# Channel projections placed between the attention steps of a hybrid layer, on one PSUM bank

## What is computed

```python
h = rms_norm(x, norm_w)
proj = jnp.einsum('bsd,de->bse', h, w_in)
q, kv_all, gate_logits, nsa_z, cv_h, cv_b, cv_c, cv_z = jnp.split(proj, SPLIT_POINTS, axis=-1)
...
o_nsa = (gates[..., 0:1] * unblock(o_cmp) + gates[..., 1:2] * unblock(o_slc)
         + gates[..., 2:3] * unblock(o_win))
o_nsa = o_nsa.reshape(B_, S_, D_NSA) * jax.nn.silu(nsa_z)
u = cv_c * cv_h
conv = lax.conv_general_dilated(u, conv_w[:, None, :], ...) + conv_b     # width 3, causal
o_conv = cv_b * conv * jax.nn.silu(cv_z)
mix = jnp.concatenate([o_nsa, o_conv], axis=-1)
return x + jnp.einsum('bse,ed->bsd', mix, w_out)
```

## Time and profile before

| | |
|---|---|
| time, median of 3 runs | 781.68 us (779.86 to 785.8) |
| the profiled execution | 780.35 us, its span 778.4 us |
| PE busy | 705.4 us, 91% of the span |
| DVE, ACT, POOL busy | 460.3, 370.0, 195.9 us |
| mean granted clock of PE | 0.989 |

### The profile page before, as it was taken

How to read it: one execution, slowest core, us unless ns; L and a number is a source line. 1 busy time by engine, 2 the same in 40 slices (tenths; PEclk the granted TensorE clock), 3 DMA queues, 4 the chain that set the end, 5 groups by cost and what they waited for, 6 DMA issues and landing times.

```text
span 778.4 us, 11020 instructions
## 1 busy us (share of the span) xinstructions
PE 705.4 (91%) x3951; PEld 587.8 (76%) x3951; DVE 460.3 (59%) x958; ACT 370.0 (48%) x891; POOL 195.9 (25%) x212
## 2 busy tenths in 40 slices
PE   2899999799999999999967778999999999999877
PEld 2888899698788888888856566777778777777755
DVE  4776462724200514033167888888898888888751
ACT  5643536432221111201046876767676766766640
POOL 2112635421122212222133532012111122222310
PEclk9999999999999999999987999999999999999999
DMA  6421122211111121120021200000000000000101
GB/s 204 163 82 41 48 75 60 55 55 41 41 41 55 43 53 43 52 55 13 1 81 61 103 1 0 24 5 28 28 19 10 29 28 28 28 28 29 55 28 54
DMA packets 17909, 36.75 MB, mean 47 GB/s; under 512 B 2496, under 2 KB 2752, under 8 KB 17856
## 3 DMA queue, kind: packets, MB, share of 16 engines
q1 hardware_dynamic: 17856, 36.05, 15.0%
HBM read 31.85 MB, written 4.19 MB: 46 GB/s over the span
## 4 chain that ended last, share of the span: by engine, by line
PE 64%; DVE 21%; ACT 7%; issue 4%; DMA 2%; POOL 1%; SPq 0%; ACTq 0%; DVEq 0%
PE pj L975 13%; PE pj L976 13%; PE pj L977 13%; DVE ptl L934 4%; PE po L1141 4%; PE tp L1161 4%; PE po L1142 3%; PE sc L1065 3%; PE sc L1064 2%; PE pout L975 2%; DVE nmax L927 2%; ACT pth L637 2%; DVE p_sel L915 2%; PE pout L976 2%; PE pout L977 2%
## 5 line engine op out<-in xcount | busy, mean ns | idle before, releaser
L368 POOL TENSOR_TENSOR wl<-raw,wh 128x512 fp32r<-128x512 f32 (+1 forms) x68 | 92.2, 1368 | 255.7 <-ACT wh L454 255.7
L975 PE MATMUL pj<-hh,wh 128*128 128x512 f32 x352 | 137.2, 390 | 0.0
L977 PE MATMUL pj<-hh,wl 128*128 128x512 f32 x352 | 137.0, 389 | 0.0
L976 PE MATMUL pj<-hl,wh 128*128 128x512 f32 x352 | 136.9, 389 | 0.0
L637 ACT CAST pth<-tp 128x512 fp32r<-128x512 f32 (+1 forms) x148 | 86.4, 587 | 78.1 <-PE tp L1161 77.0
L934 DVE TENSOR_TENSOR ptl<-tp,pth 128x512 fp32r<-128x512 f32 (+1 forms) x148 | 101.6, 687 | 30.3 <-ACT pth L637 28.5
L426 POOL TENSOR_SCALAR p_win<-p_win,precip,gate 128x64 f32<-128x64 f32 x64 | 36.6, 572 | 195.3 <-DVE precip L909 195.1
L1141 PE MATMUL po<-pth,val 128*128 128x512 f32 x132 | 64.7, 490 | 19.8 <-DVE ptl L934 17.7
L975 PE MATMUL pj<-wh,hh 128*128 128x256 f32 (+1 forms) x256 | 75.7, 296 | 7.0 <-POOL wl L368 5.8
L454 ACT CAST wh<-raw 128x512 fp32r<-128x512 f32 (+1 forms) x68 | 41.9, 626 | 80.2 <-PE pj L977 76.1
L977 PEld LDWEIGHTS pj<-hh,wl 128*128 128x128 f32 x352 | 66.1, 188 | 13.9
(11 more groups left out here) (173 smaller groups left out, 1434.1 us busy)
## 6 DMA issues: line engine op xcount, KB each, us to landing
raw<-in_wpack SPq DMA_DIRECT2D x64, 256.0 KB, 2.7
ub<-in_x SPq DMA_DIRECT2D x8, 512.0 KB, 3.4
wor<-in_wout SPq DMA_DIRECT2D x8, 512.0 KB, 3.3
xo<-in_x SPq DMA_DIRECT2D x16, 256.0 KB, 2.6
out<-xo SPq DMA_DIRECT2D x16, 256.0 KB, 2.0
raw<-in_wpack SPq DMA_DIRECT2D x4, 280.0 KB, 3.1
mixc<-in_normw SPq DMA_DIRECT2D x1, 512.0 KB, 6.3
maskb<-in_maskc SPq DMA_DIRECT2D x1, 448.0 KB, 5.6
```

Of the source, the lines that this page charges most:

```text
L368: nc.gpsimd.tensor_tensor(wl[e % 2][:, j * w:(j + 1) * w], raw[p % 4][:, 0:w], wh[e % 2][:, j * w:(j + 1) * w].bitcast(F32), ALU.subtract)\
L975: MM(dst, lh, rh, start=start, stop=False)
L976: MM(dst, lh, rl, start=False, stop=False)
L977: return MM(dst, ll, rh, start=False, stop=stop)
```

## The change

ENTRIES ends with the first z. The second z and the channel entries become 18 side tiles of 128 columns (TILES), each two groups of eight products, one for each half of the tokens. They are done in the attention steps, on the one bank `pf`, which the output projection uses after them. SIDE says how many products stand in each step, before and after the turned tiles; the loop behind it then puts together whole groups in the first 88 steps: one group of eight before the first scores, then one in every second step up to 33, and one in every third from 36 to 87. The output projection's 128 products follow from step 89, mostly 3, 3 and 2 in a step. There are 136 steps in place of 151.

UNITS now runs from the first query tile to the last. The weights of the side tiles come in halves of 512 columns (`fraw`, two buffers; `fh` and `fl`, three). ACT rounds one half in each step with a group, POOL subtracts. The first tap of the convolution is ACT's now, two remain with DVE. The output weights are loaded and split in steps 88 to 91, two in each, the second of each two by DVE. The last output tile takes its channel half first for both column halves. The key transposes of the window stand between the items of the first z. Memory is laid out anew, and the 280-column entry comes in five pieces.

```diff
-UNITS = [(i, g) for i in reversed(range(NT)) for g in range(GROUPS)]
+UNITS = [(i, g) for i in range(NT) for g in range(GROUPS)]
...
+SIDE = [(2, 2)] * 34 + [(2, 1), (2, 1), (2, 0)] * 18 + [(0, 0)] + [(1, 1)] * 4
+SIDE += [(2, 1), (2, 1), (2, 0)] * ((NS - len(SIDE)) // 3 + 2)
+SIDE = SIDE[:NS + 6] + [(4, 0)] * 4
+
+behind = 0
+for step in range(88):
+    behind += sum(SIDE[step])
+    SIDE[step] = (behind // 8 * 8, 0)
+    behind %= 8
...
+            def side(f):
+
+                kind, t, _ = TILES[f // 2]
+                cols = slice(f % 2 * 512, (f % 2 + 1) * 512)
+                if kind in ("z", "cz"):
+                    act.wait_ge(f_done, f + 1)
...
+                    A(th[:, :], pf[:, :], ACT.Tanh, scale=0.5).then_inc(f_tanh, 1)
+                elif kind == "ch":
+                    act.wait_ge(f_done, f + 1)
+                    nc.scalar.copy(mixc[:, t, cols], pf[:, :]).then_inc(f_free, 1)
+                elif kind == "cc" and f % 2 == 1:
+                    act.wait_ge(f_free, f + 1)
+                    A(mixc[:, t, :], ub[:, 2:2 + SEQ], ACT.Identity, scale=prm[:, P_CW + 3 * t + 2:P_CW + 3 * t + 3],
+                      bias=prm[:, P_CB + t:P_CB + t + 1]).then_inc(conv_first, 1)
...
                 for kind, _ in turned[:1]:
                     prob_hi(kind)
+                for f in side_ends(k, 0):
+                    if f < NF:
+                        side(f)
                 u = output_at(k)
...
+                for h in halves_at(k):
+                    half_hi(h)
+                for j in wout_at(k):
+                    act.wait_ge(wor_in[j % 2], 16 * (j // 2 + 1))
+                    act.wait_ge(f_done, NF)
+                    nc.scalar.copy(woh[:, KT_ORDER[j], :], wor[j % 2][:, :]).then_inc(woh_ready, 1)
...
+            def channels(p):
+
+                f, k = divmod(p, 8)
+                n, hf = divmod(f, 2)
+                if k == 0 and f >= 1:
+                    pe.wait_ge(f_free, f)
...
+                ins = three(pf[:, :], fh[h % 3][:, c], fl[h % 3][:, c], hh[:, k, s], hl[:, k, s], k == 0, k == NK - 1)
...
-                m, part = part_at(k)
-                if m is not None:
-                    output(m, part)
+                for p in side_parts(k, 0):
+                    channels(p) if p < OUT_0 else output(p)
                 for t in turned[1:]:
                     turn(n, *t)
+                for p in side_parts(k, 1):
+                    channels(p) if p < OUT_0 else output(p)
                 if k + 1 < NS:
                     scores(k + 1)
```

More of the change, by code:

```diff
@@ L47 @@
 ENTRIES = [("q", 0, 256, 0), ("kc", 512, 256, 0), ("q", 256, 256, 1), ("w1", 0, 256, 0),
[L48 to L52, removed]
+           ("kv", 768, 256, 0), ("w1", 1, 256, 1), ("kv", 1024, 280, 1), ("z", 1304, 256, 0)]
 NE = len(ENTRIES)
@@ L119, in output_at, with side_parts, side_ends, step_of @@
     return unit_at(k, 13)
[L122 to L132, removed]
+SIDE = [(2, 2)] * 34 + [(2, 1), (2, 1), (2, 0)] * 18 + [(0, 0)] + [(1, 1)] * 4
[6 more added lines that the diff above has]
+    behind %= 8
+SIDE_FIRST = 8
+SIDE_AT = [SIDE_FIRST]
+for a, b in SIDE:
+    SIDE_AT += [SIDE_AT[-1] + a, SIDE_AT[-1] + a + b]
+STEPS = len(SIDE)
+NX = NF + 2 * NT
+assert SIDE_AT[-1] == 8 * NX, (SIDE_AT[-1], 8 * NX)
+def side_parts(k, group):
+    return range(SIDE_AT[2 * k + group], SIDE_AT[2 * k + group + 1])
+def side_ends(k, group):
+    return [p // 8 for p in side_parts(k, group) if p % 8 == 7]
+def step_of(p):
+    return next(k for k in range(STEPS) if p < SIDE_AT[2 * k + 2])
+def halves_at(k):
+    out = []
+    for h in range(3, NHALF):
+        n = h // 2
+        p = 16 * (n - 1) + (11 if h % 2 else 0)
+        if p >= SIDE_FIRST and step_of(p) == k or p < SIDE_FIRST and k == 0:
+            out.append(h)
+    return out
+OUT_0 = 8 * NF
+KT_ORDER = (4, 5, 6, 7, 0, 1, 2, 3)
+LAST = NT - 1
+def out_part(p):
+    m, part = divmod(p - OUT_0, 16)
+    n, k = divmod(part, 8)
+    if m == LAST:
+        k, n = part // 8 * 4 + part % 4, part // 4 % 2
+    return m, n, k, KT_ORDER[k]
+def out_ends(k, group):
+    return [2 * m + n for m, n, kk, _ in (out_part(p) for p in side_parts(k, group) if p >= OUT_0) if kk == 7]
+def mixc_half_at(k):
+    for m in range(NT):
+        if step_of(OUT_0 + 16 * m - (5 if m else 1)) == k:
+            return m
+    return None
+def mixn_half_at(k):
+    for m in range(NT):
+        if step_of(OUT_0 + 16 * m + (4 if m == LAST else 0)) == k:
+            return m
+    return None
+CONV_STEPS = [step_of(16 * n + 15) for n in range(NTILES) if TILES[n][0] == "cc"]
+WOUT_STEP = step_of(OUT_0 - 1) + 1
+def wout_at(k):
+    return [j for j in range(NK) if WOUT_STEP + j // 2 == k]
 def transposes_until():
@@ L146, in transposes_until, with hybrid_layer @@
     return at, pv
[L149 removed]
+def hybrid_layer(nc: bass.Bass, x, wpack, wside, wout, normw, qnorm, knorm, par, const, maskc, out):
     with ExitStack() as ctx:
@@ L639, in prob_hi @@
                 ptn += 1
+            queries(0)
+            side(0)
             for k in range(STEPS):
@@ L946, in _ @@
                     scale(k - 1)
+                for f in side_ends(k, 0):
+                    if f < NF:
+                        side(f)
+                for c in out_ends(k, 0):
+                    residual(c)
                 u = output_at(k)
@@ L1034, in compressed, with key_transposes @@
                     .then_inc(cmp_done, 1)
-            def key_transposes(n0, normed):
+            def key_transposes(first, last, n0, normed):
                 pe.wait_ge(keys_normed, normed)
-                for n in range(4):
+                for n in range(first, last):
                     g, hf = divmod(n, 2)
```

509 lines of the change are left out of this document (309 added, 200 removed).

## The result

The changed kernel takes **842.96 us** (median of four runs, 838.06 to 844.11) where the kernel before took 781.58 in the same session: ratio 1.077, 95% interval 1.070 to 1.083. It is slower, by 61 us, 23 more than forecast. The profiled execution has a span of 840.7.

What follows compares the result with a forecast made beforehand. TensorE was taken to bound the kernel, held by ACT's order behind whole groups: 714 without waits + 40 + 37 + 15 + 6 (rest) + 6 (start and end) = 818 us of span, forecast 820, range 778 to 850.

Steps and rivals of the forecast that it cites:

- break-even at 64: Whole span: 714 us without waits against 778.4 before, so new waits of 64 us would cancel the gain.
- Front, own work, tail: Span without waits: front ends at 196.3, TensorE's own work 514 us, tail 3.5; together 714 us.
- A group between two steps: Steps 1 to 33: TensorE waits after each of 17 whole groups for work queued behind it, 40 us in all.
- ACT's kinds: Groups evicted through ACT (z, ch, cz): wait 2.4 to 2.8 us with a turned tile, 1.8 to 2.25 without.
- DVE's kinds: Groups evicted by DVE (cc first half, cb): wait 1.35 us with a turned tile, 0.45 without.
- cc second halves: Groups with ACT's first convolution tap ahead: wait 3.6 us, 0.7 more with output-unit copies; 5 us in steps 34 to 87.
- Steps 34 to 87: Two plain steps between groups and a tile in nearly each: 37 us of waits.
- The output weights: Steps 88 to 91: four load, cast and subtraction rounds of some 7 us each make TensorE wait 15 us.
- the first: Rival: groups cover what they interrupt, 0.8 us a group, weights half hidden: 763, with offset 766; chance 0.12.
- second: Rival: the sizes cancel, 1.4 us a group throughout, weights 8, rest 8: 779, with offset 782; chance 0.13.
- The third, the clock: Rival: TensorE's clock falls too, eight stretches of 13.7 us costing 5 us each: 860; chance 0.15.
- the bank as the only wait: Alternative sum by the skill's bank rule: some 0.3 us a group, 11 us, giving 752 in place of 818.

Runs made afterwards that it cites:

- e9_best: Changed kernel with side products spread over steps again and output weights loaded and split one in each of steps 88 to 95: 771.93 us.
- e8_noscale: Changed kernel with DVE's scaling of the probabilities cut to two columns, all waits and other work kept: 844.5 us.
- spread kernel: Changed kernel without the loop that puts groups together, so each group is spread over two or three steps: 765.08 us.
- e10_hold: Changed kernel with, in steps with a group, the value products of the tile before placed behind the group on TensorE: 804.01 us.

## Why the prediction came out as it did

**The direction and its reason hold.** The forecast of 820 rested on 104 us of waits against a break-even at 64. The waits are 93; the clock, which it had at nothing, cost 34.6. 840.7 - 818 = 22.7 is 34.6 less the 11 that the waits fell short, within 1 us. So two terms were off in opposite ways, and that the time lies no further from 820 is in part luck. By stretches, wait and clock together are 48.8 for 40 up to step 33, 54.2 for 37 up to step 87, 17.7 for 15 at the output weights, and 6.7 for 12 in all that is left.

**Front, own work, tail.** The front was said to end at 196.3, and the windows above have TensorE busy up to there; the only wait ahead of the first score is then 0.7 us at the query transposes. Own work 508 and 507.8. The tail waits 3.3 for 4, and what is left beside it and the three terms below is 3.4 where 8 was said.

**A group between two steps.** Said: 4.0 to 4.4 us from slot end to the next group for ACT's kinds with a tile. Measured for the four ch groups of steps 7 to 33: 3.90, 3.87, 3.90 and 3.61. Without a tile a wait of 1.8 to 2.25 was said, 1.52 to 1.79 measured. A wait of 1.35 for DVE's kinds: 1.42 and 0.75 for cc first halves, 1.30, 1.30 and 1.19 for cb. The cz kinds came out above: 3.1 and 3.8 of wait and clock against 2.4 to 2.8, and so did the cc second halves, 4.6 and 5.2 against 4.3. The sum for steps 1 to 33: 40 said, 34.8 measured. ACT's waits ahead of its reads of pf, some 4 us each by the forecast, were longer, 5 on average for the tanh and 7 for the copy (six and four waits from 200 to 370).

**What was wrong within it** is the naming of the cause. The text has it that "it is the order on ACT that holds PE". The runs give ACT's order 18 of the 78 us that grouping costs, and the order on TensorE, value products ahead of the group, 39. The arithmetic of the gap was right since it added both; but the largest term in it was the round trip of 2.0 us that the earlier trace rows shows, which a group could have covered and did not.

**Steps 34 to 87.** 37 said, 42.1 measured. The cc second halves had 5 each; 6.2 and 5.8 were found, wait and clock together. ACT's kinds had 16 in all, 30.7 was found with the clock and the output units in it: four of those gaps are 4.6, 4.6, 4.2 and 4.9 us, each with 2.7 to 4.3 us at the low clock.

**The output weights.** 15 said, with rounds of some 7 us, the seventh piece at 29 us behind the last group's end and 14.5 us of TensorE's work up to its product. The rounds are 7.0 us, the product starts at 646.18, 29.4 us behind the slot's end at 616.8, and the work up to it is 14.8: 14.6 us over, as said. Of these 5.3 are low clock and 9.3 wait; the forecast had all as wait. Since the rounds set the time here, the low clock mostly took the place of wait and added little. What came out otherwise is ACT's side: it waited six times for the loads, 9.0 us in all with 2.6 the longest, not "three times, some 5 us each".

**Of the rivals** the first (763 to 766) and second (782) fell. The third, the clock, is half true on top of the forecast: it had eight stretches of 13.7 us at 5 us each, there were 16 of 3.4 or 6.8 us, together 68 us and 34.6 of cost. The step of the forecast that failed is the clock, put at nothing because "at four fifths busy it held 2.4": that was read from the mean of a long stretch in the earlier trace rows, 45.87 of 57.60 us, in which no wait of TensorE was over 1.9 us. The runs showed 34.6 us in its place. The one bank was rightly taken as covered: its waits, 0.9 us up to 617, are less than even the 11 that the forecast set for the bank as the only wait. But e9_best shows a case for the rule of the Trainium skill, "PSUM — Partial Sum Buffer", section "Summary: rules for kernel authors", that matmuls go to another bank than the one being read: with one bank only, a group that follows at once waits 1.0 to 1.95 us each time.

## What to carry to other kernels

Where one engine's long block of independent work stands in an order with short chains that go through other engines, ask of each chain which part of it the block lies over: put the start of a round trip (here the transposes) ahead of the block and its end behind it, and the block pays for the trip; both on one side, and each block costs the whole trip. Spread blocks do this by themselves in every step. Make groups on one bank end where other work follows. Price the low clock with the waits, as about half of the time spent in it, but not where something else than TensorE sets the pace.

## What the runs showed of the hardware

**The clock fell behind a wait of 3.8 us, and behind shorter ones.** The longest wait for ACT in steps 0 to 33, behind the first cc second half, in windows (columns as above):

```profile
253.20:266.60 13.40, 8.49 (x43) 6.73 (x42) 4.86 (x15) 4.74 (x14) 1.24 (x2) 1.00 0.00 0
266.70:269.90 3.20, 3.20 (x12) 2.77 (x12) 3.10 (x7) 1.75 (x6) 0.79 (x2) 0.50 0.31 82
```

The same place in TensorE's timeline:

```profile
266.38 0.43 PE L1263 MATMUL sc<-kend,qh 128*128 128x192 f32 x1 [3.82 <-ACT qp L790]
...
268.71 0.63 PE L1175 MATMUL pf<-hh,fl 128*128 128x512 f32 x1
269.13 0.63 PE L1173 MATMUL pf<-hh,fh 128*128 128x512 f32 x1
```

TensorE had been busy for 8.49 of 13.40 us, with the wait of 3.82 at their end, and ran at 1.2 GHz for 3.4 us from 266.6 on, products 0.42 us apart in place of 0.23. Before, the fall in the attention steps lasted 13.7 us; here most last 3.4 and lie in the group behind the gap, where every product pays. Ahead of twelve of the 16 falls no wait in the last 13 us was over 2.4 us; ahead of that at 321.1 there were 1.21 and 0.63. The Trainium skill, "TensorE: Matmul & The Clock Gate", section "HAM oscillation — how this bites in real kernels", describes bursts that each start at the low clock behind a wait for DMA of 3 to 5 us, at a cost of half the throttled time. The trace agrees on the cost, 34.6 of 68, or some 31 with the correction above; here the waits were for other engines, and most of them were shorter. That one cut in DVE's work (e8_noscale) left the time alone and gave 82 us of low clock suggests that it also depends on how the gaps happen to fall.

**DVE's work between two places in SBUF is held up by POOL.** In the spread kernel DVE's subtraction of output weights beside POOL's (timeline):

```profile
546.01 2.37 POOL L566 TENSOR_TENSOR wol<-wor,woh 128x1024 fp32r<-128x1024 f32 x1
...
546.83 2.63 DVE L1156 TENSOR_TENSOR wol<-wor,woh 128x1024 fp32r<-128x1024 f32 x1 [0.37 <-ACT woh L832]
```

The same in e9_best, with POOL idle:

```profile
550.13 1.23 DVE L1165 TENSOR_TENSOR wol<-wor,woh 128x1024 fp32r<-128x1024 f32 x1
```

It takes 1.23 alone, and 2.63 where POOL is at work, ending 1.08 us behind POOL. The other three of the spread kernel start 0.2 to 0.8 us before POOL ends, take 1.32 to 1.82, and end 1.08 us behind POOL too. DVE's scaling of 256 columns does the same in e10_hold, 1.08 at 309.76 under a POOL subtraction for 0.41 at 283.99 with POOL idle, while its subtractions that read PSUM stay at 0.67 to 0.69. The Trainium skill, "SBUF — State Buffer", section "SBUF: two separate sides", says that DVE and GpSimd share a pair of ports as an exclusive lock; these rows agree. What it costs this kernel as a whole was not tried.

**Open.** Steps 34 to 87 keep 30 us of waits with whole groups in the best order found. The spread kernel shows that they go when every step has products; which of them is a tile's round trip, and which the start of a unit (`tp` for POOL's `qp`, 6.1 us in three waits) or the output unit, no run here tells apart.
